# Ten of 24 conditioning matrix pieces multiplied on VectorE, with their weights interleaved into the first weight stream

## The reference

```
h = rmsnorm(x, norm_mix); z = h @ w_in                      # 1024 x 2048
y = concat(rmsnorm(b * conv3(c * v)), rmsnorm(real(fft2(u))))
x = x + y @ w_out
q = rmsnorm(x) @ w_q;  k = rmsnorm(mem) @ w_k;  v = rmsnorm(mem) @ w_v
x = x + softmax(q k^T) v @ w_o
x = x + moe(rmsnorm(x))                                     # 32 experts, top 4
...
for each of 4 sublayers of the second block:                # (layer, 0) and (layer, 1)
    m = silu(c) @ ada_w + ada_b                             # c: 1 x 1024, ada_w: 1024 x 3072
    shift, scale, gate = split(m)
```

## Time and profile before

| | |
|---|---|
| runs of the kernel | 2105.39, 2086.86, 2086.72 us; median 2086.86 us |
| profiled execution | 2106.02 us, of which the trace spans 2104.2 us |
| PE / DVE / ACT / POOL busy | 1881.5 / 751.7 / 538.4 / 140.7 us |
| mean granted TensorE clock | 0.935 |
| HBM read | 585.29 MB, 279 GB/s over the span |

### The profile page before, as it was taken

The page is one execution under the profiler, slowest core; times in us unless marked ns, Lnnn a source line. Parts: engine busy times, 40 slices in busy tenths (PEclk is TensorE's granted clock), DMA queues, the critical chain, the costliest instruction groups (busy, mean ns, idle before and its releaser), DMA issues.

```text
span 2104.2 us, 25272 instructions
## 1 busy us (share of the span) xinstructions
PE 1881.5 (89%) x10270; PEld 1155.1 (55%) x10270; DVE 751.7 (36%) x1136; ACT 538.4 (26%) x700; POOL 140.7 (7%) x49
## 2 busy tenths in 40 slices
PE   6998898999999999999999999755699979568997
PEld 6855665434444344433443344634589868357996
DVE  3323232111111111111111111477565476656555
ACT  4322341111111111111111111335334432533442
POOL 0100110000000000000000000240300030311000
PEclk9998895999999999999999999866799989888999
DMA  8488568899999999999999999440145535213450
GB/s 310 166 303 331 177 227 334 356 417 417 419 418 417 417 419 418 417 417 419 418 417 417 419 418 416 156 159 1 60 154 185 200 120 192 88 60 117 164 179 21
DMA packets 136599, 587.07 MB, mean 279 GB/s; under 512 B 6446, under 2 KB 6660, under 8 KB 102756
## 3 DMA queue, kind: packets, MB, share of 16 engines
q1 hardware_dynamic: 135108, 581.25, 70.0%
q10 hardware_dynamic: 1440, 5.11, 0.7%
HBM read 585.29 MB, written 1.05 MB: 279 GB/s over the span
## 4 chain that ended last, share of the span: by engine, by line
PE 62%; DMA 20%; DVE 13%; ACT 3%; issue 2%; SPq 0%; POOL 0%; ACTq 0%; DVEq 0%
PE bank L1047 29%; DMA ring<-in_w_gate_up 20%; PE bank L1255 14%; PE bank L1279 5%; PE bank L1215 3%; PE bank L1118 2%; PE bank L1288 1%; DVE sb_X L1992 1%; PE bank L1108 1%; DVE arena_r L2021 1%; DVE sb_XN L1962 1%; PE bank L1246 1%; PE bank L1381 1%; PE bank L1272 1%; DVE sb_XN L1933 1%
## 5 line engine op out<-in xcount | busy, mean ns | idle before, releaser
L1255 PE MATMUL bank<-ring,arena 128*64 128x512 f32 x2048 | 458.6, 598 | 8.0 <-DMA ring<-in_w_gate_up 8.0
L1255 PEld LDWEIGHTS bank<-ring,arena 128*64 128x64 f32 x2048 | 140.3, 137 | 321.0 <-issue 298.5
L1047 PE MATMUL bank<-w_hi,arena_r 128*128 128x512 f32 (+1 forms) x784 | 259.5, 393 | 6.5 <-DVE arena_r L2037 3.7
L1279 PE MATMUL bank<-ring,arena 128*64 128x512 f32 x1024 | 226.8, 595 | 0.0
L487 DVE TENSOR_TENSOR w_lo<-ring,w_hi 128x4096 fp32r<-128x4096 f32 (+2 forms) x37 | 161.6, 4367 | 134.0 <-ACT w_hi L477 133.8
L477 ACT ACTIVATE w_hi<-ring 128x4096 fp32r<-128x4096 f32 (+2 forms) x45 | 160.6, 3577 | 131.3 <-PE bank L1047 130.7
L1047 PEld LDWEIGHTS bank<-w_hi,arena_r 128*128 128x128 f32 x784 | 149.3, 190 | 37.2 <-DVE arena_r L2037 4.1
L487 POOL TENSOR_TENSOR w_lo<-ring,w_hi 128x4096 fp32r<-128x4096 f32 (+1 forms) x8 | 70.6, 8821 | 1366.2 <-ACT w_hi L477 1365.8
L825 ACT ACTIVATE arena<-arena,sb_tab 128x512 f32<-128x512 f32 x32 | 23.1, 722 | 530.0 <-DVE arena L1826 530.0
L1047 PE MATMUL bank<-XT_r,w_hi 128*128 128x256 f32 x512 | 147.8, 289 | 12.0 <-DVE arena_r L2021 12.0
L1800 DVE TENSOR_SCALAR arena<-sb_tab,sb_pos 128x64 f32<-128x64 f32 x66 | 13.8, 252 | 400.0 <-PE bank L1255 400.0
(11 more groups left out here) (318 smaller groups left out, 2376.3 us busy)
## 6 DMA issues: line engine op xcount, KB each, us to landing
ring<-in_w_gate_up SPq DMA_DIRECT2D x128, 2048.0 KB, 23.1
ring<-in_w_down SPq DMA_DIRECT2D x64, 2048.0 KB, 22.3
ring<-in_mlp_w SPq DMA_DIRECT2D x32, 2048.0 KB, 8.2
ring<-in_ada_w SPq DMA_DIRECT2D x24, 2048.0 KB, 9.4
ring<-in_c_w_in SPq DMA_DIRECT2D x6, 2048.0 KB, 7.6
ring<-in_w_in SPq DMA_DIRECT2D x4, 2048.0 KB, 7.6
ring<-in_w_k SPq DMA_DIRECT2D x2, 2048.0 KB, 12.2
ring<-in_w_v SPq DMA_DIRECT2D x2, 2048.0 KB, 21.2
```

The costliest lines, as they stand in the source:

```text
L1047: mm = pe.matmul(out, st[a], mv[b], start=start and a + b == 0, stop=stop and a == 1, skip_group_check=True)
L1255: mm = pe.matmul(B[m][CAP * h:CAP * h + CAP, :], xe[:, 2 * j + kl, :], w[:, kl, m * D + h * HW:m * D + (h + 1) * HW], start=False, stop=(j ...
L1279: mm = pe.matmul(B[2][CAP * h:CAP * h + CAP, :], hT[:, c, CAP * j:CAP * j + CAP], w[:, c, h * HW:(h + 1) * HW], start=False, stop=(j == 1 ...
```

## The change

- `ada` units 0 to 9 are no longer multiplied by PE. DVE does them (`ada_on_dve`): one tensor_scalar and seven scalar_tensor_tensor instructions of 128 x 512, each waiting for the one before, accumulate weight row block k times the k-th column of the conditioning vector in `acc_v`. PE then adds the 128 partitions with four 1-column matmuls (`combine_v`), and DVE adds the bias (`ada_v_done`).
- Their loads move into the first part of the stream: units 0 to 7 between the granules of `w_k`, `w_v` and `w_in`, units 8 and 9 behind the two of `w_out`. The ring stays at four slots.
- The small loads (router weights and bias, positions, sinks, the Fourier table) are issued behind granule 8 and not behind granule 3.
- `CT` and `U` lie in `XN`, since the accumulators of units 4 to 7 take their place. PE's semaphore `used` skips the granules of DVE. Several semaphores of the second block are merged into `ab_T` and `ab_Te`, with the same order.

```diff
-ADA_AT = [("mix_in", 5), ("fft", 3), ("yfft", 2), ("mixss", 2), ("mix_out", 2), ("q", 1), ("scores", 3),
-          ("w_o", 2), ("router", 4)]
+NV = 10
+ADA_AT = [("mixss", 2), ("mix_out", 2), ("q", 1), ("scores", 3), ("w_o", 2), ("router", 4)]
...
-    out = [("w_k", i) for i in range(2)] + [("w_v", i) for i in range(2)] + [("w_in", i) for i in range(4)]
-    u = 0
-    tail = {"mixss": [("w_out", 0), ("w_out", 1)], "mix_out": [("w_q", 0), ("w_q", 1)],
+    out = [("w_k", 0), ("w_k", 1), ("ada", 0), ("ada", 1), ("w_v", 0), ("ada", 2), ("ada", 3), ("w_v", 1), ("ada", 4),
+           ("w_in", 0), ("ada", 5), ("w_in", 1), ("ada", 6), ("w_in", 2), ("ada", 7), ("w_in", 3)]
+    u = NV
+    tail = {"mixss": [("w_out", 0), ("ada", 8), ("w_out", 1), ("ada", 9)], "mix_out": [("w_q", 0), ("w_q", 1)],
...
+                elif o in ON_DVE:
+                    sp.wait_ge(sem("adav_acc"), ON_DVE.index(o) + 1)
...
-                if g == 3:
+                if g == 8:
...
+            def combine_v(*us):
+                for u in us:
+                    pe.wait_ge(sem("adav_acc"), u + 1)
+                    if u >= 8:
+                        pe.wait_ge(sem("adav_done"), 8)
+                    for c in range(4):
+                        mm = pe.matmul(B[5][:, 4 * u + c:4 * u + c + 1], acc_v[u][:, c * P:(c + 1) * P],
+                                       ones[:, 0:1], start=True, stop=True)
+                    mm.then_inc(sem("adav_comb"), 1)
...
+            def ada_on_dve(u):
+
+                g = ON_DVE[u]
+                dve.wait_ge(landed[slot_of(g)], FILL[g])
+                w = slot(slot_of(g)).rearrange("p (k n) -> p k n", k=KC)
+                if u >= 8:
+                    dve.wait_ge(sem("adav_comb"), u - 7)
+                link(dve.tensor_scalar(acc_v[u], w[:, 0, :], sil[:, 1, 0:1], None, ALU.mult))
+                for k in range(1, KC):
+                    ins = dve.scalar_tensor_tensor(acc_v[u], w[:, k, :], sil[:, 1, k:k + 1], acc_v[u], ALU.mult, ALU.add)
+                    if k < KC - 1:
+                        link(ins)
+                ins.then_inc(sem("adav_acc"), 1)
...
-            half_lo(dve, "w_k", 0, 1, 2, 3)
-            half_lo(dve, "w_v", 0, 1, 2, 3)
+            half_lo(dve, "w_k", 0, 1)
+            ada_on_dve(0)
+            ada_on_dve(1)
+            half_lo(dve, "w_k", 2, 3)
+            ada_on_dve(2)
+            for h in range(4):
+                half_lo(dve, "w_v", h)
+                ada_on_dve(3 + h)
...
             half_lo(dve, "w_in", *range(2, 8))
+            ada_on_dve(7)
...
-            half_lo(dve, "w_out", 0, 1, 2, 3)
+            half_lo(dve, "w_out", 0, 1)
+            ada_v_done(*range(8))
+            ada(2)
+            ada_on_dve(8)
+            half_lo(dve, "w_out", 2, 3)
+            ada_on_dve(9)
```

More of the change, by code:

```diff
@@ L121 @@
 SPLIT = [p for p in PRE if p[0] != "ada"]
+ON_DVE = [PRE.index(("ada", u)) for u in range(NV)]
 PER_E = 6
@@ L309, in build_program @@
         QT = ext[:, 6144:8192].rearrange("p (k s) -> p k s", k=KC)
-        CT = arn(0, 1024)
-        U = arn(1024, 1024).rearrange("p (t n) -> p t n", t=TB)
+        acc_v = [ext[:, 6144 + HW * (u % 8):6144 + HW * (u % 8) + HW] if u % 8 < 4 else arn(HW * (u % 8 - 4), HW)
+                 for u in range(NV)]
+        CT = XN[:].rearrange("p t d -> p (t d)")[:, 0:1024]
+        U = XN[:].rearrange("p t d -> p (t d)")[:, 1024:2048].rearrange("p (t n) -> p t n", t=TB)
         SQ = arn(2048, 2048).rearrange("p (k s) -> p k s", k=8)
@@ L729, in ada @@
                     unit[0] += 1
-                    act.wait_ge(*done("ada", u))
+                    act.wait_ge(*done("ada", NV + u))
                     if u >= 2:
@@ L1020, in _, with used_up @@
             at = [0]
+            def used_up(mm):
+                g = at[0] + 1
+                while g in ON_DVE:
+                    g += 1
+                mm.then_inc(used, g - at[0])
+                at[0] = g
             def granule(w=SLOT):
@@ L1065, in half_done @@
             def half_done(mm):
[L1067 to L1068 removed]
+                if n_half[0] % 2:
+                    mm.then_inc(sem("half_used"), 1)
+                else:
+                    used_up(mm)
             def chunk_ready(st, k):
@@ L1171, in _ @@
             mm.then_inc(sem("mix_ss"), 1)
+            combine_v(*range(2, 8))
+            pe.wait_ge(sem("cs"), 1)
             ada(2)
@@ L1535, in _ @@
                 mm = pe.transpose(B[5][:, t * P:(t + 1) * P], R2b[:, t, P:2 * P], ident)
-            mm.then_inc(sem("k_T"), 1)
-            for m, (st, src, e) in enumerate((("i_", R4b, "a_Te"), ("b_", R1b, "k_Te"))):
+            mm.then_inc(sem("ab_T"), 1)
+            for m, (st, src, e) in enumerate((("i_", R4b, 2), ("b_", R1b, 5))):
                 pe.wait_ge(sem(st + "rope"), 2)
-                pe.wait_ge(sem(e), 2 + m)
+                pe.wait_ge(sem("ab_Te"), e)
                 s2 = src[:, 0:1024].rearrange("p (t n) -> p t n", t=TB)
@@ L1544, in _ @@
                                           s2[:, t, j * P:(j + 1) * P], ident)
[L1545 to L1548, removed]
+                mm.then_inc(sem("ab_T"), 1)
+            pe.wait_ge(sem("ab_Te"), 7)
+            pe.wait_ge(sem("ab_Te"), 5)
+            pe.wait_ge(sem("ab_Te"), 9)
             def q_ab(a):
@@ L1663, in ada, with to_mod, ada_v_done @@
                     unit[0] += 1
-                    a, nb = u // 6, u % 6
                     dve.wait_ge(sem("ada_comb"), u + 1)
-                    dve.scalar_tensor_tensor(mod[:, a, 4 * nb:4 * nb + 4], B[7][:, 0:4], float(nb >= 2),
-                                             ada_bT[:, 24 * a + 4 * nb:24 * a + 4 * nb + 4], ALU.add,
-                                             ALU.add).then_inc(sem("ada_done"), 1)
+                    to_mod(NV + u, B[7][:, 0:4]).then_inc(sem("ada_done"), 1)
+            def to_mod(u, src):
+                a, nb = u // 6, u % 6
+                return dve.scalar_tensor_tensor(mod[:, a, 4 * nb:4 * nb + 4], src, float(nb >= 2),
+                                                ada_bT[:, 24 * a + 4 * nb:24 * a + 4 * nb + 4], ALU.add, ALU.add)
+            def ada_on_dve(u):
[10 more added lines that the diff above has]
+                ins.then_inc(sem("adav_acc"), 1)
+            def ada_v_done(*us):
+                dve.wait_ge(sem("adav_comb"), us[-1] + 1)
+                for u in us:
+                    to_mod(u, B[5][:, 4 * u:4 * u + 4]).then_inc(sem("adav_done"), 1)
             def add_residual(st, base, w):
```

54 lines of the change are left out of this document (24 added, 30 removed).

## The result

The changed kernel takes 2138.77 us (median of 4 runs, 2132.63 to 2142.84); the kernel before, run beside it, 2095.78 us (4 runs, 2086.72 to 2105.39). The ratio is 1.0202, 95% interval 1.0134 to 1.027. In a second set, on another chip, it was 2134.56 against 2103.2 us, ratio 1.0154 [1.0106, 1.0202]. So it is slower by 31 to 43 us by the medians; 40 were forecast. Both intervals lie above 1, so the loss is clear of the noise, but whether it is over 2% is not settled. The kernel before has two groups of times, near 2087 and from 2095 to 2109 us, and its median moves with how many runs fall in each. Its profiled executions span 2130.8 and 2137.8 us, that of before 2104.2 us.

The account below looks back on a forecast made before the run. The prediction took the kernel as PE-bound nearly everywhere in the first 360 us. Its terms, 54.6 - 23.3 + 5.3 + 3.7 = +40.3 us, moved the median from 2086.86 to 2127 us, range 2106 to 2147.

Parts of the forecast that it names:

- slow side of before: Rival: loads 2 us slower at four waits, or median on slow side of 18.7 us: +48 to +59 us, chance 0.22.
- Term 1: First projections: DVE's units and their ring loads move the end of `w_in` from 121.1 to 175.7 us, +54.6.
- walk of the ring: First projections: step-by-step times of unit loads, freed slots and DVE's subtractions, with `w_in` starting at 126.9 us.
- no lock: Rival: DVE and POOL don't get in each other's way, both 4.5 us fall away: +31 us, 2118 us, chance 0.15.
- Terms 2 and 3: Mixer to `w_out`: changes on PE's path, -23.3 us; clock +5.3, made of +4 at half clock and +1.3 in `w_out`.
- The 1.3 us for `w_out`'s first half: Clock part at `w_out`: its first half runs slower after a longer wait, +1.3 us (bounds 0 and 1.5).
- Term 4: Behind `w_out`: combines of units 8 and 9 ahead of the next transposes, at half clock, 2 x 1.87, +3.7 us.
- Behind the memset: After POOL's first memset of the router, which marks `w_o`'s end: later work unchanged, only shifted, 0 us.
- Full clock: Rival: the clock stays up through combines and after waits: +30 us, with no lock too +21, 2108 us; chance 0.13.
- In-time loads: Rival: DVE's units are hidden and loads come in time, given a free slot: -8 us, 2079 us, chance 0.10.

Follow-up runs that it names:

- e8: e3, but each of the first eight DVE units made in two parts of four row blocks, stream order fitted, small loads behind `w_v` 1: 2082.74 us, ratio 0.9915.
- e3: e1 with PE's combines of units 2 to 7 moved behind units 10 and 11: 2080.61 us, ratio 0.9908 to the kernel before.
- b2: The kernel before, unchanged, run and profiled once more: 2099.78 us.
- e1: Changed kernel with the same work and loads, eight units placed elsewhere in the weight stream and DVE's program: 2090.9 us, ratio 0.9938 to the kernel before.
- e4: Changed kernel with units 0 to 7 not loaded, DVE multiplying a resident table instead, small loads back behind granule 3: 2096.01 us, ratio 0.9989.
- e9: e3 with only four combines ahead of `w_out`, those of units 6 to 9 between `w_q`'s transposes and projection: 2081.19 us, ratio 0.9902.

## Why the prediction came out right

The forecast was 2127 us, from a sum of +40.3. The change itself came out as +43.0 and +31.4 us by the medians of the two sets. The measured 2138.77 lies 11.8 us above 2127, and 8.9 of these are the base: 2086.86 was the median of three runs, and with a fourth beside it that median was 2095.78. The range held it in its upper part, which was left for the slow side of before. So the closeness of +40.3 to +43.0 is partly luck, while the stages below are what the mechanism is judged by. Up to the memset +37.0 was measured, and +33.6 between the spans of before and of the changed kernel's second profile, which have the same router stage (60.2 us).

**Term 1 (+54.6; measured +52.8).** The walk of the ring held to within 3 us at each step, and it was luck that its errors cancelled in part:

| step | forecast | measured |
|---|---|---|
| unit 2 issued | 43.1 | 44.17 |
| unit 4 landed | 74.7 | 76.28 |
| unit 5 landed | 88.5 | 91.37 |
| `w_v` half 3 split | 100.9 | 99.5 |
| unit 6 landed | 113.9 | 112.52 |
| unit 6 done | 124.0 | 122.84 |
| `w_in` starts | 126.9 | 125.86 |
| `w_in` lasts | 48.8 | 48.04 |

Three sizes were off. A unit is 5.92 us, not 5.6: scalar_tensor_tensor, here with the multiplier read from a column, starts every 0.79 us, where the earlier trace rows gave 0.73, behind a TENSOR_TENSOR. That is 0.3 us for each of the units on the path. Unit 5 landed 15.1 us after unit 4 where the walk had 13.8; the small loads held the stream for 4.6 us and not 3.3. SP had issued them and `w_in` 0 only by 76.22, when unit 4 was about to land (76.28), and from 77 to 78 us the DMA engines move 2 GB/s. And `w_in` took 0.8 us less than forecast. And one step was wrong: that POOL splits the first half of `w_in` when PE has left `w_v` half 2, beside unit 5. ACT's high part was indeed written at 92.9 to 94.8, but a subtraction also waits for the low part before it:

```
eng.wait_ge(sem("w_hi"), n)
if n > 1:
    eng.wait_ge(sem("w_lo"), n - 1)
```

That low part is DVE's, behind unit 5. So the two can't meet there, in any timing; it took off 4.5 us and hid the 2.9 us by which the load was late. The other meeting, beside unit 6, came as forecast and cost 4.4 us (4.89 against 0.49). The rival "no lock" was half right, for a reason in the program and not in the timing.

**Terms 2 and 3 in the mixer (-23.3 and +4; measured -18.9).** The parts agree: 2.5 us to the transform, 7.12 us for it, 3.7 for the group transforms (3.4), 3.56 for the sums, 5.90 for six combines (5.9), then 3.61 and 3.67 for units 10 and 11, at the half clock that I took. The granted clock, 0.93 while the six combines ran, is 0.50 from 200 to 208 us, the lower of its two levels. From the combines' start to `w_out` it was 25.6 us against 21.5 + 4. That DVE's `mod` stands behind two subtractions is in the chain (212.99 and 215.38). **The 1.3 us for `w_out`'s first half** did not come: it took 23.25 us, 23.52. That term was mis-sized: it is nothing, or 0.3 us the other way.

**Term 4 (+3.7; measured +3.1 from `w_out` to `w_q`).** The two combines take 3.41 us at half clock. The loads behind stayed hidden.

**Behind the memset** I had set 0. From the first long product of the experts to the second block (ACT's `sb_XN` at 1325.32 before, 1352.35 after) it took 948.3 and 948.4 us; in the three profiles of before 951.0, 950.5 and 949.8; in e8 948.4 and in e3 950.8. No run tells why. The router stage, from the memset to the experts, takes 48.9 to 60.2 us: 60.2 in all three profiles of before, 53.0 and 60.2 in the two of the changed kernel, and 48.9 to 60.2 in the others. This, and the 6 us of b2, are most of the spread of either kernel's runs that profiles show; why some runs of before take 2087 us stays open.

**The rivals.** "Full clock" falls by the 3.6 us units; of its three parts the one for `w_in` was a quarter right (0.8 of 2.9 us). "In-time loads" did not happen, but e1 and e8 show that its numbers were of the right size: forecast -8 if DVE is hidden and loads come in time, measured -9.3 at the memset in e1 against the first profile of before, and -3.2 against b2. With the combines moved as well it is -17.7 in e3 and -23.6 in e8 (-11.6 and -17.5 against b2). It was said to decide at unit 2's load, which must start well before half 3 of `w_k` is split: in e1 it is issued at 25.86, and that half is split at 42.2.

```profile
25.86 0.37 SPq L528 DMA_DIRECT2D ring<-in_ada_w  x1
...
37.50 4.68 DVE L466 TENSOR_TENSOR half_lo<-ring,half_hi 128x2048 fp32r<-128x2048 f32 x2
```

## What to carry to other kernels

When work is moved to an engine with idle time, walk the ring: note for each load which instruction frees its slot, and for each subtraction which load it now stands behind. Here, at the end of `w_in`, the work cost 15 us, the loads 26 and both together 53; the same work and loads in another order cost 7, and in half pieces with a stream to fit 1.5. An added piece is to fit the free time between two instructions that the bottleneck waits for, and go behind the one that is wanted next. And read every wait in a helper before you lay two engines beside each other: one `w_lo` wait decided that a collision could not happen.

## What was not expected of the hardware

- An instruction of 0.49 us took 4.89 us when it met POOL's subtraction of 4.49 us, though it has only one tensor input in SBUF and a column. In the prediction I had laid the meeting to the seven instructions with two inputs, which did stretch in e4 (9.70 for 5.48). By the Trainium skill, SBUF — State Buffer, section Who interferes with whom, tensor_scalar can enter a two-port mode and then contends too; the 0.49 us for 512 elements, against 0.76 for scalar_tensor_tensor, agrees with such a mode, though no run here separates it. DVE's row begins 0.04 us before POOL's in the trace, and DVE was the one held up all the same. Copies out of a bank were not stretched beside POOL's subtractions: four take 2.48 us in e1 and e4, where they overlap one, and 2.48 in the changed kernel, where they don't.
- One-column combines cost 0.98 us each in a run of six at a granted clock of 0.93 (5.90 us), and 1.7 in the same number behind a wait, at 0.50 (10.24 us). In e9 they ran at that price in both places, also at 0.50; in e3 six took 9.06 us.
- Half clock falls in different places in executions of one program. From 146 to 166 us the granted clock was 0.91, 1.00 and 1.00 in the three profiles of before, from 166 to 187 us 0.82, 0.89 and 0.76; they reach the memset at 314.1, 313.9 and 308.0 us.
